# Two-layer hybrid decoder trunk: x transposed without its norm weights, memory split once, root chains apart, attention's end in quarters

## The reference

```python
h = rms_norm(x, norm_mix[l])
q, k, v = split(h @ w_in[l])            # 16 heads of 64: 4 differential, 6 dilated, 6 block-sparse
q, k = rotary(rms_norm(q, gain)), rotary(rms_norm(k, gain))      # first quarter of each head turned
o_a = rms_norm((softmax(q1 k1) - lam * softmax(q2 k2)) @ v, subln) * (1 - lam_init)
o_b = dilated mixture;  o_c = causal attention
x = x + concat(o_a, o_b, o_c) @ w_out[l]
m = rms_norm(mem, norm_mem[l]) @ w_mkv[l]                         # 256 memory rows
x = x + softmax(rms_norm(rms_norm(x, norm_cross) @ w_mq) k_m) v_m @ w_mo[l]
x = x + (silu(g) * u) @ w_down[l],  g, u = rms_norm(x, norm_ffn) @ w_gate_up[l]
```

## Time and profile before

| | |
|---|---|
| three runs | 776.17, 776.72, 777.16 us (median 776.72) |
| the profiled execution | 777.14 us, span 775.3 us |
| PE busy | 715.5 us (92%), 3836 matmuls |
| DVE, ACT, POOL busy | 501.0 (65%), 383.6 (49%), 115.6 us (15%) |
| the gate/up/down loops | 219 to 385 us and 600 to 766 us, PE busy 166.0 us in each |
| layer 0 before its loop, layer 1 between the loops | 0 to 219 us, 385 to 600 us |

### The profile page before, as it was taken

How to read it: one execution, slowest core, us unless ns; L and a number is a source line. 1 busy time by engine, 2 the same in 40 slices (tenths; PEclk the granted TensorE clock), 3 DMA queues, 4 the chain that set the end, 5 groups by cost and what they waited for, 6 DMA issues and landing times.

```text
span 775.3 us, 10608 instructions
## 1 busy us (share of the span) xinstructions
PE 715.5 (92%) x3836; PEld 600.9 (78%) x3836; DVE 501.0 (65%) x829; ACT 383.6 (49%) x562; POOL 115.6 (15%) x102
## 2 busy tenths in 40 slices
PE   3969989898899999999989699998899999999997
PEld 2857777787788888888868577776788888888885
DVE  4595686554667766667578667753737666676664
ACT  5744766446354443454446367572636434544432
POOL 5550022206200000000034300402160000000000
PEclk9998999997899999999999899998969999999999
DMA  8864332222355666665558424313252667556741
GB/s 291 309 234 150 122 109 82 82 70 94 109 164 162 196 213 187 202 176 162 198 207 272 163 82 136 109 55 102 63 160 66 192 181 205 171 163 207 210 124 54
DMA packets 122158, 120.84 MB, mean 156 GB/s; under 512 B 2928, under 2 KB 95232, under 8 KB 122128
## 3 DMA queue, kind: packets, MB, share of 16 engines
q1 hardware_dynamic: 119744, 113.26, 46.9%
q0 software_dynamic: 1664, 5.86, 2.1%
q10 hardware_dynamic: 720, 1.33, 0.5%
HBM read 119.39 MB, written 1.05 MB: 155 GB/s over the span
## 4 chain that ended last, share of the span: by engine, by line
PE 75%; DVE 9%; ACT 8%; POOL 4%; issue 3%; DMA 1%; ACTq 0%; DVEq 0%; POOLq 0%
PE ps L1666 19%; PE ps L1359 14%; PE ps L1671 10%; PE ps L1699 5%; PE ps L1700 5%; PE ps L1701 5%; PE ps L1327 3%; PE ps L1684 3%; ACT whi L559 2%; DVE wlo L837 2%; ACT sq L633 2%; PE ps L1622 2%; PE ps L1426 1%; PE ps L1469 1%; PE ps L1481 1%
## 5 line engine op out<-in xcount | busy, mean ns | idle before, releaser
L837 DVE TENSOR_TENSOR wlo<-raw,whi 128x2048 fp32r<-128x2048 f32 (+1 forms) x101 | 232.2, 2317 | 57.3 <-ACT whi L559 56.8
L559 ACT ACTIVATE whi<-raw 128x2048 fp32r<-128x2048 f32 (+1 forms) x108 | 200.7, 1875 | 26.6 <-PE ps L1359 14.6
L1666 PE MATMUL ps<-both,whi 128*128 128x512 f32 x640 | 159.2, 391 | 0.0
L1666 PEld LDWEIGHTS ps<-both,whi 128*128 128x128 f32 x640 | 117.6, 188 | 22.7
L1359 PE MATMUL ps<-whi,both 128*128 128x512 f32 x448 | 120.2, 403 | 4.5 <-DVE both L881 3.4
L1359 PEld LDWEIGHTS ps<-whi,both 128*128 128x128 f32 x448 | 83.0, 192 | 24.3 <-DVE both L881 3.9
L1671 PEld LDWEIGHTS ps<-both,wlo 128*128 128x128 f32 x640 | 87.3, 190 | 6.2
L788 ACT ACTIVATE qkv<-ps 128x512 f32<-128x512 f32 x44 | 26.4, 599 | 132.7 <-PE ps L1671 122.4
L1671 PE MATMUL ps<-both,wlo 128*128 128x256 f32 x640 | 89.2, 282 | 0.0
L1699 PE MATMUL ps<-whi,ahi 128*128 128x512 f32 x176 | 69.2, 393 | 1.6 <-DVE alo L1259 1.6
L1700 PE MATMUL ps<-wlo,ahi 128*128 128x512 f32 x176 | 69.0, 392 | 0.0
(11 more groups left out here) (176 smaller groups left out, 904.7 us busy)
## 6 DMA issues: line engine op xcount, KB each, us to landing
raw<-in_w_gate_up SPq DMA_DIRECT2D x88, 512.0 KB, 5.0
raw<-in_w_in SPq DMA_DIRECT2D x24, 1024.0 KB, 5.5
raw<-in_w_down SPq DMA_DIRECT2D x22, 1024.0 KB, 4.9
raw<-in_w_out SPq DMA_DIRECT2D x8, 1024.0 KB, 5.0
raw<-in_w_mkv SPq DMA_DIRECT2D x4, 1024.0 KB, 5.2
xn<-in_mem POOLq DMA_DIRECT2D x2, 1024.0 KB, 5.5
raw<-in_w_mq SPq DMA_DIRECT2D x4, 512.0 KB, 3.4
raw<-in_w_mo SPq DMA_DIRECT2D x2, 1024.0 KB, 4.7
```

The costliest lines, as they stand in the source:

```text
L559: act.activation(whi[s][:, 0:n], raw[s][:, 0:n], ACT.Copy).then_inc(hi_done[s].sem, 1)
L837: dve.tensor_tensor(wlo[s][:, 0:n], raw[s][:, 0:n], whi[s][:, 0:n].bitcast(F32), ALU.subtract)\
L1666: pe.matmul(ps[:, bank, :], whi[s][:, a:a + P], both[:, :, k, :], start=(k == 0), stop=False)
```

## The change

- x: `gain_x`, xn and the broadcast weights are gone. PE transposes xs itself; in the transposed form a norm weight is one number for a partition, so `x_hi` and `x_lo` apply it, in four operations of 128x128 for a quarter. PE waits for each half tile of the new x (`x_new` counts halves).
- Memory: loaded, transposed and split once, in slots 18 to 21 of layer 0, into mhi and mlo of their own; its norm weights go into the splits of w_mkv, in four operations of 128x512.
- Roots: `norm_part(e)` takes a chain for each of q, k, q, k; `CHAIN_AT` has four slots, the queries' ones a chunk before the keys'.
- Attention's end: head outputs are scaled four heads at a time (the last four from banks 0 and 1), three of four pairs are transposed within the slots, and the second half of w_out is done in half pieces (`out1_half`), nine of them in slots 93 to 101.
- The low parts of w_out's four units go from DVE to POOL (`DVE_LO`).
- Start: the identity and x's first tile first, unit 0 in four pieces, then x's second tile.
- In the memory attention both maxima are taken before the root is waited for, and the split of the first gate/up unit stands behind the exponentials; output products and sums go by halves.

```diff
             def x_hi(layer, b, q):
 
                 act.wait_ge(t_ps.sem, t_ps.at(layer, 4 * b + q + 1))
-                act.activation(quarter(thi, q), bank_as_chunks(X_BANKS[b][q]), ACT.Copy).then_inc(t_hi.sem, 1)
+                if layer == 0 and b == X_MIX and q == 0:
+                    act.wait_ge(s_rows.sem, 16)
+                for k in range(4):
+                    c, tok, gain = chunk_of_x(layer, b, q, k)
+                    ins = act.activation(thi[:, c, tok], ps[:, X_BANKS[b][q], k * P:(k + 1) * P], ACT.Copy, scale=gain)
+                ins.then_inc(t_hi.sem, 1)
...
-            def scale_qk(half):
-
-                    dve.wait_ge(reduced.sem, reduced.at(layer, 2 * half + 2))
+                def norm_part(e):
+
+                    part, half = e % 2, e // 2
+                    dve.wait_ge(reduced.sem, reduced.at(layer, e + 1))
...
+                    rsqrt(T * n)
...
+                    dve.tensor_tensor(z, z, r.unsqueeze(3).to_broadcast((P, T, w, HD)), ALU.mult).then_inc(scaled.sem, 1)
...
-                pool.wait_ge(mem_in.sem, mem_in.at(layer, 16))
-                pool.wait_ge(s_gain.sem, s_gain.at(layer, 16))
-                if layer == 0:
-                    pool.wait_ge(s_memss.sem, 1)
-                pool.tensor_tensor(xn[:], xn[:], g_mem[:].unsqueeze(1).to_broadcast((P, T, D)), ALU.mult)\
-                    .then_inc(xm_ready.sem, 1)
...
+                for u in range(DVE_LO, U_MQ):
+                    split_lo(layer, u)
...
                 for t in range(T):
-                    add_to_x(layer, 0, t, (U_OUT + 3,), lambda t, c: OUT1_BANKS[t][c])
-                    gain_tile(layer, 0, t, g_cross)
+                    add_to_x(layer, 0, t, lambda t, c: OUT1_BANKS[t][c])
...
-CHAIN_AT = (26, 66)
+CHAIN_AT = (14, 26, 52, 62)
-DVE_LO = U_MQ
+DVE_LO = U_OUT
```

More of the change, by code:

```diff
@@ L777, in _ @@
                         x_hi(layer, X_FFN, q)
+                for t in range(T):
                     squares_of_x(layer, 2, t)
@@ L903, in add_to_x @@
                                                        xs[:, t, cols], ALU.mult, ALU.add)
-                ins.then_inc(x_new.sem, 1)
-            def gain_tile(layer, stage, t, gain):
-                dve.wait_ge(x_new.sem, x_new.at(layer, 2 * stage + t + 1))
-                for c in range(2):
-                    gain_x(gain, 2 * t + c)
+                    ins.then_inc(x_new.sem, 1)
             def lambdas():
@@ L1114, in _ @@
                         diff_out()
-                    for half in range(2):
-                        if g == CHAIN_AT[half]:
-                            scale_qk(half)
                     if layer == 0 and g == LAM_AT:
@@ L1643, in mo_acc, with output @@
                     return ps[:, 2 * t + c, :]
-                products(layer, U_MO, (0,), mo_acc, chunks=2, first=True, last=True, done=False, cols=D,
-                         built=(om_hi, om_lo, 1)).then_inc(t0_done.sem, 1)
+                def output(t, columns):
+                    s = U_MO % RING
+                    if t == 0:
+                        pe.wait_ge(hi_done[s].sem, hi_done[s].at(layer, fill(U_MO) + 1))
+                    pe.wait_ge(om_hi.sem, om_hi.at(layer, t + 1))
+                    tok = slice(t * P, (t + 1) * P)
+                    for c in columns:
+                        for part, (x_part, w_part) in enumerate(((thi, whi), (thi, wlo), (tlo, whi))):
+                            if t == c == 0 and part == 1:
+                                pe.wait_ge(lo_done[s].sem, lo_done[s].at(layer, fill(U_MO) + 1))
+                            if c == 0 and part == 2:
+                                pe.wait_ge(om_lo.sem, om_lo.at(layer, t + 1))
+                            for k in range(2):
+                                a = k * D + 512 * c
+                                ins = pe.matmul(mo_acc(t, c), x_part[:, k, tok], w_part[s][:, a:a + 512],
+                                                start=part == k == 0, stop=part == 2 and k == 1)
+                        if (1, t, c) in SUMS:
+                            ins.then_inc(summed.sem, 1)
+                        else:
+                            ins.then_inc(used[s].sem, 1)
+                output(0, (0,))
                 pe.wait_ge(om_ready.sem, om_ready.at(layer, 2))
                 transpose_pair(om, 1, 7, SEQ, omT_ps)
-                products(layer, U_MO, (1,), mo_acc, chunks=2, first=True, last=True, cols=D, built=(om_hi, om_lo, 2))
+                output(0, (1,))
+                output(1, (0, 1))
                 for q in range(4):
@@ L1849 @@
     w = {n: put(n, inputs[n]) for n in WEIGHTS}
-    gains = {n: put(n, inputs[n]) for n in GAINS}
+    rows = np.stack([np.asarray(inputs[n]) for n in GAINS], axis=1).reshape(DEPTH, len(GAINS), KC, P)
+    gains = {}
     rot = np.stack([rotated("qn"), rotated("kn")], axis=1)
```

433 lines of the change are left out of this document (247 added, 186 removed).

## The result

The changed kernel takes 749.05 us (median of four executions, 747.05 to 749.81), the kernel before, run beside it, 776.44 (774.51 to 777.16). The ratio is 0.9647, 95% interval 0.9621 to 0.9673. The profiled execution took 749.81 us, its span is 748.0, so 27.3 us less than before; the forecast was 30.7.

A forecast was written before the change was run, and what follows sets the result against it. PE, busy 92% of the span, was taken as the bound, with some 55 us of waits nearly all outside the gate/up/down loops. Gains of 37.8 less 7.1 gave 30.7 us, so 746.0 us; likeliest 741 to 752, range 733 to 759.

The forecast's parts named there:

- The start: Up to PE's first low-weight piece: earlier identity and x's first tile gain 2.0 us, between nothing and about 4.
- Queries and keys: Before the first scores: the queries' early chain leaves short keys' waits, saving 9.4 us in layer 0, 7.9 in layer 1.
- Memory once: Memory: layer 1's 16 transposes and both layers' waits for its low part go, 5.0 us; gains on weights hidden.
- the attention's end: Last heads' transposes: quarters built early leave only about 0.7 us of wait, saving 3.3 us a layer, 6.6.
- new waits: Attention: heads' quarters 3.5 us, late combines 2.4, plus 1.2 before second memory query tiles: a cost of 7.1 us.
- Norm weights in the copies: Copies of x: four waits of 5.1 us go, short operations cost 0.5 before each gate/up; net 4.7, 1.2 costed separately.
- First memory softmax: Memory attention: moved weight split and both maxima before the root save 1.1 us a layer, 2.2.
- the clock holds: Rival: in the memory attention PE stays at 2.4 GHz, up to 5 us a layer, 736; 17%.
- POOL's splits: Four output units: low-part splits of 4.5 us each on POOL, costed at nothing; as a rival 782, 3%.
- the signs: What would show the forecast true, here POOL near 36 us busier by splits less 11 of memory products.
- DVE becomes the pace: Rival: extra root chains make keys 3 us later a layer and softmax waits three times larger, 11 us back, 757; 23%.
- The wait moves only: Rival: the keys' wait is as long as the queries' was and brings the low clock, 760 or more, to 766; 5%.

The follow-up runs named there:

- the late chains: Changed kernel with the queries' root chain directly ahead of the keys' (slots 26 and 62), both transposes together at slots 38 and 75: 768.39 us.
- x first: Changed kernel with x's second tile loaded ahead of unit 0's four pieces and x's high parts made on ACT ahead of unit 0's: 741.19 us.
- together: Changed kernel with x's second tile before unit 0, queries' transposes in slot 33, first w_mkv split later, idle transposes in waits, heads' transposes in 74/76: 728.88 us.
- slot 33: Changed kernel with the queries' first transposes in slot 33 instead of 30: 748.70 us.

## Why the prediction was right, and where its steps were not

The time, 749.05, lies 3 us above the forecast of 746.0 and inside its likeliest span. The sum of 30.7 was 27.3, and its parts were off by more than that: the two stretches before the first scores gave 6.5 us less than forecast, layer 1's memory attention 2.7 more by the clock. That the sum came so near is in part luck.

**The start (2.0 forecast).** Wrong. The first low-weight piece comes at 17.5 to 18.9 us in nine programs with this start, 18.14 on average over eight of them, 18.11 before. I had put "nothing" as the lower bound and chosen the identity's early landing; the second tile behind the pieces took it back. Its place costs about 2 us at that piece.

**Queries and keys (17.3).** Right in its mechanism, which the late chains confirm (7.1 us in layer 0). In layer 0 no wait is left where I had counted 1.9, but not because DVE was early. My own bounds gave 1.9 to 3.6 (51.3 to 53 for the keys, PE there at 49.4), and I took the low end. The keys were ready at 54.31, later than that, and PE came at 54.36, 5.0 us later than I counted, by its late start and the low clock at 18.7 to 22.1 us. That part is luck: with x first the wait is 0.47 us, in "together" 1.31. In layer 1 the failing step is "counted the same way the keys' wait is 1.3 us": the queries' wait came first, 2.52 us and as much as 1.8 of low clock, from two turning steps of POOL behind DVE's splits. I had used this lock to explain the 5.10 us split of before and not looked for it in the new order. With slot 33 the keys' wait was 0.94, near my 1.3.

**Memory once (5.0), the attention's end (6.6), new waits (7.1).** Together the attention stretches gave 7.6 for a forecast of 7.3. The combines wait 2.1 us in all (2.4 forecast), the last high part 0.69 (0.7), the heads' second transposes 0.93 (0.55), the first none (0.7). But the largest waits are the 2.08 and 0.87 us behind the four-operation splits of w_mkv, which I had called hidden ("on ACT about 0.6 us more"). The 0.6 was right (2.54 us, 1.91 in one operation); what failed is "hidden": the place of the split makes the rest of the wait, and two slots later it is 0.2.

**Norm weights in the copies (4.7, less 1.2).** The size of the price is the miss. I took 0.5 us before each gate/up; PE waits 2.08 us there where it waited 0.69, with the low clock behind it, and there is a wait of 0.67 at the layers' border that I had not counted. Over the kernel the short operations cost some 11 us. The stretches before the loops became shorter all the same, because the wait of 1.23 us for the product is gone, and one of 0.56 before the output's products.

**First memory softmax (2.2).** The wait for the first exponentials fell from 1.75 to 1.16 us in both layers, 0.6 of the 1.1. The stretches gained 3.2 in layer 1 and 0.4 in layer 0. That is not the softmax but the rival *the clock holds*, which came true in one layer of the two. I had given it 17% as one event; it is a throw of the dice for each place. Undoing the split's place cost nothing.

**POOL's splits.** At nothing, and nothing it was. They take 36.8 us more of POOL's time, and 11.2 us of memory products are gone, as the signs said.

**The rivals.** "DVE becomes the pace" did not show in the time, though the keys came 1.3 to 3 us later than I counted in layer 0. "The wait moves only" happened in layer 1 alone, at 2.52 us.

The clock behind it all: after like waits the granted clock fell in one execution and held in another, 0.50 against 1.00, at 2.8 us for a memory attention and 1.6 at the border. The Trainium skill ("TensorE: Matmul & The Clock Gate", section "What's actually happening") says that how many matmuls run cold varies from run to run of one kernel. The executions agree: with the low parts on DVE they took 740.72 us at a mean granted clock of 0.995, 748.5 at 0.984 and 751.49 at 0.976. What decides it in a single case no run here shows.

## What to carry to other kernels

Compare two traces by stretches between the same instructions, not by the median alone: here an edit that won 3.1 us in its place showed nothing in the time, and one worth about 2 us showed 7.9, because behind short waits of PE elsewhere the low clock came or did not. If such waits can't be removed, idle transposes in them may help: the four kernels that have them spread over 1.7 to 4.5 us (the one time of 2475 us aside), the edits without over 2.1 to 10.8 us. And when work is put on GpSimd, look at every two-input operation of VectorE beside it in the new order, not only at the one that was slow in the old.

## What had not been expected of the hardware

- PE's idle time costs twice at random: behind a wait of about 1.2 us before the first transposed probabilities the granted clock was 0.50 for some 10 us in layer 0 and stayed at 1.00 in layer 1 of the same execution. With twelve idle transposes in these waits it was 1.00 there in both layers of four kernels.
- DVE's variance step on 128x8 numbers took 1.60 us beside POOL's split of 4.58 and 0.17 without it; POOL's steps of 0.46 and 0.32 us took 2.38 and 2.41 beside DVE's splits of 2.28.
- Four copies with a scale column of 128x128 take 1.06 us on ACT, and four subtractions on DVE as much; the start's loads landed up to 1.5 us apart in programs that are the same up to there.
